# Differential scores and maxima map by map, layer 0's tiles in turn, the first tile of layer 1 projected in plain fp32

## The reference, cut to what matters

```python
branch = concat([mix, mem_o]) * silu(gate)          # block 1, layers A and B
x = x + branch @ w_out[i]
# block 2, layers 0 and 1
h  = rms(x, g_pre) * (1 + scale) + shift            # hc likewise, from the context
s1 = einsum('bqhd,bkhd->bhqk', q1, k1) * 48 ** -0.5 # 4 heads, 48 columns a map
s2 = einsum('bqhd,bkhd->bhqk', q2, k2) * 48 ** -0.5 # keys: 512 latent + 256 context
w  = softmax(s1) - lam * softmax(s2)
o  = einsum('bhqk,bkhe->bqhe', w, v)                # 96 columns a head
b_out = rms(o, subln_g) * (1 - lam_init)
y = concat([a_out * silu(na_g), b_out * silu(df_g), c_out * silu(cv_g)]) @ w_out
x = x + gate * rms(y, g_post)                       # context likewise in layer 0
```

## Time and profile before

| what | value |
|---|---|
| median of 3 runs | 1652.66 us (1650.25 to 1654.98) |
| profiled execution | 1653.44 us, of which the span is 1651.6 us |
| DMA | 161.36 MB, mean 98 GB/s |
| instructions | 22948 |
| largest groups of PE | L2596 575.2 us (x1696), 359.1 us (x1360), 224.5 us (x720) |
| projection in plain fp32, L3139 | 58.4 us (x128), mean 602 ns |

### The profile page before, as it was taken

One profiled execution on the slowest core, in us unless ns is written; L12 is line 12 of the kernel. 1 busy time (PEld: TensorE's weight loads), 2 busy tenths in 40 slices (PEclk: granted clock), 3 DMA queues, 4 the chain that ended last, 5 costly groups with the idle time before them and its releaser, 6 DMA issues.

```text
span 1651.6 us, 22948 instructions
## 1 busy us (share of the span) xinstructions
PE 1597.0 (97%) x8870; PEld 1277.7 (77%) x8870; DVE 979.8 (59%) x1803; ACT 667.6 (40%) x1323; POOL 140.7 (9%) x192
## 2 busy tenths in 40 slices
PE   7999999899999999999999999989999999999898
PEld 6977877687878878878888888865656887788676
DVE  1356454456556655665447787565665467876674
ACT  3365443424323323263313435244554325433653
POOL 4132100000000000002000110000112001000001
PEclk9999999899999999999999999999999999999899
DMA  8221244334654764462223111221003134213100
GB/s 289 81 77 50 103 153 117 80 82 121 190 158 120 155 185 139 148 151 68 92 96 109 56 54 40 92 93 58 1 26 96 48 107 140 58 39 128 52 14 39
DMA packets 171252, 161.36 MB, mean 98 GB/s; under 512 B 40374, under 2 KB 154280, under 8 KB 171112
## 3 DMA queue, kind: packets, MB, share of 16 engines
q1 hardware_dynamic: 151944, 126.97, 26.1%
q10 hardware_dynamic: 16928, 25.27, 4.7%
q0 software_dynamic: 2272, 7.64, 1.4%
HBM read 149.80 MB, written 11.18 MB: 97 GB/s over the span
## 4 chain that ended last, share of the span: by engine, by line
PE 83%; DVE 10%; ACT 4%; issue 2%; DMA 0%; POOL 0%; ACTq 0%; SPq 0%; POOLq 0%; DVEq 0%
PE psum L2596 46%; PE psum L2567 10%; PE psum L2630 7%; PE psum L3139 5%; PE psum L2621 4%; PE psum L3137 2%; PE psum L2775 2%; PE psum L2687 2%; PE psum L2730 2%; DVE arena L1999 1%; PE psum L2669 1%; PE psum L3010 1%; DVE arena L1969 1%; DVE wring_r L2076 1%; DVE arena L2133 1%
## 5 line engine op out<-in xcount | busy, mean ns | idle before, releaser
L2596 PE MATMUL psum<-hT_r,wring_r 128*128 128x512 f32 x1696 | 575.2, 393 | 3.6 <-ACT branch L1745 1.1
L2596 PEld LDWEIGHTS psum<-hT_r,wring_r 128*128 128x128 f32 x1696 | 319.3, 188 | 79.0 <-issue 10.0
L2596 PE MATMUL psum<-arena_r,wring_r 128*128 128x256 f32 (+1 forms) x1360 | 359.1, 333 | 0.7 <-ACT branch L1564 0.5
L1564 ACT ACTIVATE arena<-psum 128x512 f32<-128x512 f32 (+6 forms) x256 | 149.8, 611 | 416.0 <-PE psum L2596 244.2
L2596 PEld LDWEIGHTS psum<-arena_r,wring_r 128*128 128x128 f32 x1360 | 218.3, 190 | 26.2 <-issue 1.8
L2567 PE MATMUL psum<-arena 128*128 128x96 f32 (+9 forms) x1460 | 220.8, 365 | 16.9 <-ACT branch L1745 7.1
L2596 PE MATMUL psum<-arena_r 128*128 128x512 f32 (+1 forms) x720 | 224.5, 350 | 0.0
L2567 PEld LDWEIGHTS psum<-arena 128*128 128x128 f32 (+5 forms) x1460 | 160.8, 189 | 64.7 <-issue 31.9
L2596 PE MATMUL psum<-hT_r,arena_r 128*128 128x512 f32 x448 | 177.8, 397 | 1.8 <-DVE wring_r L2076 1.0
L2630 PE MATMUL psum<-ident,arena 128*128 128x128 f32 (+3 forms) x1104 | 145.9, 277 | 17.4 <-DMA arena<-in_c_ctx 7.4
L2630 PEld LDWEIGHTS psum<-ident,arena 128*128 128x128 f32 (+3 forms) x1104 | 125.2, 142 | 39.6 <-issue 14.6
(11 more groups left out here) (237 smaller groups left out, 1967.8 us busy)
## 6 DMA issues: line engine op xcount, KB each, us to landing
wring<-in_w_in_b SPq DMA_DIRECT2D x54, 512.0 KB, 5.9
arena<-in_w_mod ACTq DMA_DIRECT2D x16, 1536.0 KB, 8.3
wring<-in_w_in SPq DMA_DIRECT2D x16, 1536.0 KB, 6.9
wring<-in_w_out SPq DMA_DIRECT2D x8, 2048.0 KB, 8.4
wring<-in_w_in_a SPq DMA_DIRECT2D x5, 1536.0 KB, 6.6
arena<-x_dram SPq DMA_DIRECT2D x3, 2048.0 KB, 14.6
wring<-in_w_in SPq DMA_DIRECT2D x6, 1024.0 KB, 5.7
arena<-ebias_dram SPq DMA_DIRECT2D x144, 32.0 KB, 1.8
```

The lines of the kernel that those rows point to most:

```text
L1564: return nc.scalar.activation(out, in_, ACT.Copy, scale=scale)
L2596: ins_ = nc.tensor.matmul(b[0:hi.shape[2], 0:width], w[:, k], v[:, k], start=k + p == 0, stop=(k, p) == (KT - 1, 2))
```

## The change

The scores and the maxima of the differential stage are made map by map: PE claims the banks of a map and issues both parts of it, then the other map; DVE takes the maximum of the first map, combines the item before, and takes the maximum of the second map. Layer 0's tiles come in the order latent 0, context 0, latent 1, context 1, latent 2, latent 3. `oN` moves right behind what stands beside `dS`. `hcT 1` moves from behind `doT` of the last tile to behind `dT` of its last item. Layer 1's first tile is projected in plain fp32, so that its branch and its use of the split weights fall away; the splits of the output weights move from items 4 to 8 to items 8 to 11, two an item, and DVE's part of each waits until PE has read the plain weights for tile 0. `gate B 4` stands ahead of `qm B`, and `gate B 0` may start on the high parts. `nk` and `nkc` issue high by high and low by high before they wait for the state's low part. `final_rows(TT - 2)` gets a step of its own, `xr`, ahead of `hcT 0`. In layer 1 `nv` stands ahead of `nq`. The rooms of the first items' probabilities, the throwaway outputs of squares, the numbers of the norms and the allowed banks follow from the new order.

```diff
-YO_SPLITS = {4: ((0, 0), (0, 1)), 5: ((0, 3),), 6: ((0, 2), (1, 0)), 7: ((1, 1), (1, 3)), 8: ((1, 2),)}
+YO_SPLITS = {8: ((0, 0), (0, 1)), 9: ((0, 3), (0, 2)), 10: ((1, 0), (1, 1)), 11: ((1, 3), (1, 2))}
...
-    for i in range(4):
+    for i in range(5):
         add("a", "gate", "B", i)
     add("av", "qm", "B")
-    add("a", "gate", "B", 4)
     add("a" * 8, "mS", "B")
...
+    add("", "xr")
     add("vvvv", "hcT", 0)
     add("", "xf")
...
-        add(lat_ctx * 3, "nq", l)
+        if l == 0:
+            add(lat_ctx * 3, "nq", l)
         add("aaaavv", "nv", l)
+        if l:
+            add(lat_ctx * 3, "nq", l)
...
 def diff_tiles(l):
-    return ([TT + t for t in range(CT)] if l == 0 else []) + list(range(TT))
+    return [0, TT, 1, TT + 1, 2, 3] if l == 0 else list(range(TT))
+def turn_order(l):
+    return [("k", t) for t in (0, 1, TT, 2, 3, TT + 1)] + [("q", t) for t in diff_tiles(l)]
...
             add("a", "dT", l, t, h)
+            if n > len(items) and l == 0:
+                add("vvvv", "hcT", 1)
...
-            rows = [(tiles[i - 1], 1)] if h == 1 and i else [(t, 0)] if n == 5 or (h == DH - 1 and i) else []
+            rows = [(tiles[i - 1], 1)] if h == 1 and i else [(t, 0)] if h == DH - 1 and i else []
+            rows = [row for row in rows if row[0] != tiles[0]]
...
         beside(n)
+        if n >= 2 and h == 0 and i:
+            add("", "oN", l, tiles[i - 1])
...
         if n >= 2:
-            if h == 0 and i:
-                add("", "oN", l, tiles[i - 1])
...
-                if l:
+                if l and i > 1:
                     add("", "yb", tiles[i - 1], 1)
...
     add("v", "doT", l, last)
-    if l == 0:
-        add("vvvv", "hcT", 1)
-    else:
+    if l:
         add("", "yx", l, before)
...
                 elif kind == "yv":
                     dve.wait_ge(yo_w_hi, yo_ws.index((half, q)) + 1)
+                    read_by_pe(dve, ("yo", 1, 0, half, 1))
...
                 elif kind == "dS":                      # DVE
-                    if (t, h) != diff_items(l)[0]:
-                        diff_combine(n - 1)
                     for i in range(2):
                         full(dve, key, i)
                         chained(nc.vector.reduce_max(d_max[:, p, i:i + 1], halves(t, i), AX_XY if t < TT else AX_X))
                         scaled(d_neg[:, p, i:i + 1], d_max[:, p, i:i + 1], -diff_scale).then_inc(diff_negmax, 1)
+                        if i == 0 and (t, h) != diff_items(l)[0]:
+                            diff_combine(n - 1)
...
-                    for p, (w, v) in enumerate(((hi, x_hi), (hi, x_lo), (lo, x_hi))):
+                    if turned:
+                        pe.wait_ge(hi_ready, hi_at(turned, last_k))
+                        passes = ((hi, x_hi), (lo, x_hi), (hi, x_lo))
+                    for p, (w, v) in enumerate(passes):
+                        if turned and p == 2:
+                            evacuated(pe, turned, b_)
...
                     for k in range(KT):                  # nk
+                        pe.wait_ge(hi_ready, hi_at(("hT", f"C{l}"), k))
+                        for g, (hi, lo) in enumerate(parts):
+                            nc.tensor.matmul(banks[g], hi[:, k], hT_hi[:, k], start=k == 0, stop=False)
+                        for g, (hi, lo) in enumerate(parts):
+                            nc.tensor.matmul(banks[g], lo[:, k], hT_hi[:, k], start=False, stop=False)
                         evacuated(pe, ("hT", f"C{l}"), k)
                         for g, (hi, lo) in enumerate(parts):
+                            ins_ = nc.tensor.matmul(banks[g], hi[:, k], hT_lo2[:, k], start=False, stop=k == KT - 1)
...
-                    for half in range(2):                # dS, PE
-                        claim(pe, key, half)
...
-                        for part in range(2):
-                            cut = slice(part * KEYS // 2, (part + 1) * KEYS // 2)
-                            for half in range(2):
+                        for half in range(2):
+                            claim(pe, key, half)
+                            for part in range(2):
+                                cut = slice(part * KEYS // 2, (part + 1) * KEYS // 2)
                                 ins_ = product(psum[:, 2 * half + part, 0:KEYS // 2], [(q[half], dkT[rows[half], h, cut])])
-                                if part:
-                                    done(ins_)
+                            done(ins_)
...
-                    for k in yo_rows(t, piece) if l and not turned_last else ():
+                    for k in yo_rows(t, piece) if l and t and not turned_last else ():
...
-                    for k in yo_rows(t, piece) if l == 0 else ():
+                    for k in yo_rows(t, piece) if l == 0 or t == 0 else ():
                         ins_ = nc.tensor.matmul(b, src[:, k, tt * P:(tt + 1) * P], w[:, k], start=k == 0, stop=k == 5)
```

More of the change, by code:

```diff
@@ L277, in schedule @@
                     add("a", "cT", l, h)
-        turns = [("k", t) for t in (0, 1, TT, 2, 3, TT + 1)] + [("q", t) for t in diff_tiles(l)]
+        turns = turn_order(l)
         def turn(slot):
@@ L459, in turn_banks @@
         return range(BANKS - 1)
-    if key[2] == "k" or key[3] >= TT:
-        return range(BANKS - 1)
-    slot = (6 + key[3] + CT * (key[1] == 0)) // 2 + (key[0] == "dX")
+    slot = turn_order(key[1]).index(key[2:]) // 2 + (key[0] == "dX")
     return (range(BANKS - 1), (4, 5, 6), (4, 6))[max(slot, 4) - 4]
 def diff_tiles(l):
-    return ([TT + t for t in range(CT)] if l == 0 else []) + list(range(TT))
+    return [0, TT, 1, TT + 1, 2, 3] if l == 0 else list(range(TT))
+def turn_order(l):
+    return [("k", t) for t in (0, 1, TT, 2, 3, TT + 1)] + [("q", t) for t in diff_tiles(l)]
 def diff_items(l):
@@ L932, in hybrid_stack_kernel @@
         before_mem = split_at[("Bproj", 1, 0), 0]
-        split_starts = [("wout", "A"), ("wout", "B"), ("hcT", 1)]
+        split_starts = [("wout", "A"), ("wout", "B"), ("doT", 0, TT - 1)]
         split_bounds = [sum(split_jobs(key) for key, _ in steps[:order_of[start]]) for start in split_starts]
@@ L1120, in hybrid_stack_kernel @@
         for ph in norms:
[L1121 to L1125, removed]
+            if ph not in ("C0", "C1"):
+                tiles = {"F": FINAL_NORMS, "c1": NEXT_NORMS}.get(ph, [(ph, t) for t in range(norms[ph][2])])
+                for name, i in tiles:
+                    n_tiles += 1
+                    norm_no[name, i] = n_tiles
         norm_pe, n_tiles = {}, 0
@@ L1162, in yo_at @@
         def yo_at(l, t):
-            return t - TT if t >= TT else CT + t if l == 0 else TT + CT + t
+            return l * (TT + CT) + diff_tiles(l).index(t)
         def yo_rows(t, piece):
@@ L1567, in square @@
                 src, dst, _, ss, _ = norms[ph]
-                if ph == "c1":
-                    dst = cxn1
-                nc.scalar.activation(dst[:, t], src[:, t], ACT.Square, accum_out=ss[:, t:t + 1]).then_inc(sq_done, 1)
+                junk = cxn1[:, TT - 1] if ph == "c1" else dst[:, t]
+                nc.scalar.activation(junk, src[:, t], ACT.Square, accum_out=ss[:, t:t + 1]).then_inc(sq_done, 1)
             def final_squares(key, turns):
@@ L1936, in _ @@
                     b = full(act, key, 0)
-                    junk = cxn1[:, t % TT if l == 0 else 0]
+                    junk = cxn1[:, min(t, TT - 1) if l == 0 else 0]
                     nc.scalar.activation(junk[:, half * BANK:(half + 1) * BANK], b, ACT.Square,
@@ L2590, in split_features @@
                 for k in blocks:
+                    passes = ((hi, x_hi), (hi, x_lo), (lo, x_hi))
                     if key[0] == "nkc" and i == 0 and k % 2 == 0:
-                        evacuated(pe, ("hcT", key[1]), k // 2)
-                    if new and i == 0:
-                        evacuated(pe, new, k)
-                    for p, (w, v) in enumerate(((hi, x_hi), (hi, x_lo), (lo, x_hi))):
+                        turned, last_k, b_ = ("hcT", key[1]), k + 1, k // 2
+                    else:
+                        turned, last_k, b_ = new if i == 0 else None, k, k
+                    if turned:
[4 more added lines that the diff above has]
+                            evacuated(pe, turned, b_)
                         ins_ = nc.tensor.matmul(b[0:hi.shape[2], 0:width], w[:, k], v[:, k], start=k + p == 0, stop=(k, p) == (KT - 1, 2))
@@ L3121, in _ @@
                         pe.wait_ge(last_hi, 1)
-                    elif l:
+                    elif l and t:
                         pe.wait_ge(yo_x_lo, yo_xs.index((t, piece)) + 1)
```

13 lines of the change are left out of this document (7 added, 6 removed).

## The result

The changed kernel takes 1664.05 us (median of 9 runs, 1658.97 to 1669.25) against 1653.73 us before (9 runs); the ratio is 1.006, 95% interval 1.0047 to 1.0073. The forecast was 1650, its range ended at 1661: outside the range, and on the other side. The profiled execution has a span of 1662.9 us, 11.3 more than before.

A forecast was written before the change was run, and what follows sets the result against it. PE, busy 97% of the span, was taken to bound the kernel. The terms -10.4 - 0.3 - 1.8 + 1.1 + 3.0 + 1.7 - 0.7 + 5.2 gave -2.2 us; forecast 1650 us, eight-in-ten range 1638 to 1661.

The forecast's parts named there:

- Parts 1 and 2: `gate B 4` ahead of `qm B`: -10.4 us; `nk` starting on the high parts with `xr` first, layer 0: -1.8 us.
- R4: Rival at `mS B`: the gate's eviction still meets the split in ACT's queue, `mS` waits as before; 1661 us, chance 0.04.
- Part 3: Scores and maxima map by map in the differential stages: no gain in PE's work, `oN` 1.46 us later.
- R3: Rival in the differential stages: PE runs the maps one after the other; +35 us, 1685 us, chance 0.03.
- part 4: Layer 0's differential stage with its tiles in turn, a latent tile first: +1.1 us, bounds -4 to +5.
- part 7: Layer 1's differential stage, four pieces summed: +5.2 us, bounds -3 to +9.
- (c): Layer 1's stage: DVE's weight splits, two an item in items 8 to 11, make PE wait through item 12: +4.5 us.
- Part 5: `hcT 1` in layer 0's last item delays the eviction before `yo 3`: +3.0 us and +1.7 of clock.
- Part 6: Layer 1 before the stage: `nv` ahead of `nq` gives DVE time for the splits: -0.7 us, bounds 0 to -1.5.
- (b): Layer 1's first tile in plain fp32: 0.69 us more a piece, +2.1 us beyond the piece counted in the first items.
- (a): Layer 1's first items without the splits: -4.4 us, less 1.5 for the combination before the fourth item's dT.
- R2: Rival in both stages' first items: DVE's order decides and its waits bring the clock down; about +6, 1659 us, chance 0.21.

## Why the prediction was wrong

By stretches of the profiled executions, in us against the kernel before:

| stretch | forecast | changed kernel | with DVE's old order |
|---|---|---|---|
| up to the first scores | -12.5 | -11.3 | -12.4 |
| layer 0's stage | +1.1 | +5.2 | -1.6 |
| to layer 1's first scores | +4.0 | +5.2 | +3.1 |
| layer 1's stage | +5.2 | +10.7 | -2.3 |
| the end | 0 | +1.5 | +0.1 |
| sum | -2.2 | +11.3 | -13.0 |

Each column is one execution. In the eight kernels that have the changed kernel's steps up to there the first scores of layer 0 start between 1064.63 and 1068.07 us, so 2 or 3 us in the first row say nothing.

**Parts 1 and 2 were right.** `nk 0` is 12.0 us earlier; 12.5 were forecast. R4 is out.

**Part 3 is the step that failed: it put the late combination at nothing where no projection fills PE.** Half of the mechanism stood in the text: DVE's combination now stands between the maxima, `oN` comes 1.46 us later, PE waits for it at a boundary of layer 1. The wait is 1.1 to 1.4 us. PE's side stood too: eight score records take 1.57 us map by map where they took 1.56 in turn, so the row groups overlap and R3 is out. What failed is the step "Where nothing fills PE (the first items) the loop takes 4.8 to 4.9 us by this working as before", and the sum that followed. The starts of the scores are 4.97 us apart in the changed kernel, as written. But map by map the start says only that the first map's banks are free. The second map starts 1.28 us later, and PE goes on when that is done. From the start of one item's scores to the end of the next one's it is 6.52 us before, 6.43 with the claims map by map and DVE as before, and 7.81 in the changed kernel (the rows of layer 0's stage above, at the higher level). With the claims together the starts show it as well: 6.34 instead of 4.96. Either way the order takes 1.3 to 1.4 us an item there, one wait of 1.10 us for the combination ahead of `dT` and one for the second map's exponential.

The forecast counted 1.5 us for the whole of layer 1's first items; they cost 8.9 (the first seven items take 57.99 us against 49.14 with the old order), of which the clock is 6.8: 13.7 us at the lower level against none. In layer 0 I wrote "1.0 at the boundaries" where a tile costs 1.48, because I followed `oN` and not `yx` and what waits behind it. The terms that name this order are 3.0 us in part 4 and 1.5 and 1.5 in part 7, in all 6.0; the 4.5 of part 7 (c) are for the splits with this order behind them. It measured 23.5.

**Part 4** was counted with the order in it. Without it layer 0's stage gains 1.6 us, in a profile without the 6.8 us at the lower level of the kernel before, which are worth 3.4.

**Part 5 was right**: 3.3 us of wait were forecast, 3.47 came. `nk 1` was to come 4.7 us later, the clock included; it does with DVE's old order (52.78 us from the last scores, 48.04 before), and 6.8 in the changed kernel. That the sum fits to 0.1 is luck: in that profile the lower level stretched the eight records behind the wait from 3.60 to 6.38 us, 2.8 where 1.7 were forecast, so 2 are left of the 3.0. Against `hcT 1` behind `doT` it cost 5.4.

**Part 6** is open: 0.7 forecast, 1.6 measured between `nk 1` and the scores (229.41 us against 230.97). But of the ten other kernels with `nv` ahead of `nq` four took 229.3 to 229.4 us there and six 230.9 to 231.2, so one execution doesn't show what this edit is worth.

**Part 7**: (b) is 0.69 us for each plain piece, as worked out (the pitch is 7.09 and not 6.40). Items 7 to 15 lose 7.7 us, where the three pieces of (b) that are left, (c) and (d) had 2.1 + 4.5 + 1.5 = 8.1; what was missed is the same 1.5 us once more behind the last tile. With DVE's old order they lose only 3.6, so more than half of the 7.7 is the order again. (a) is what failed: the first items were to gain 2.9 us and lost 3.0. With DVE's old order they gain 5.9, of which 5.1 is clock.

R2 named the mechanism (DVE's order decides, and its waits bring the clock down) at 1659, with a chance of 0.21. It was short as well: it priced the clock and not the waits, and in layer 0's stage the clock stayed up. Still it was nearer. The sum priced a late combination only where a tile ends, though the profile before had 12 us of PE's waits and 8.5 of lost clock in the two stages, most of them in the first items, where PE stands behind DVE and ACT.

## What to carry to other kernels

- When a reduction and the finishing pass of the item before share an engine, the finishing pass goes first: its user is the next thing that the busiest engine asks for, and it can run while the new scores are being made. Put between the two maxima, in 40 items, it cost 23.5 us here; put behind both, 5 more.
- Price a changed order of one engine against every instruction behind it in its queue, in each regime of the loop (filled, unfilled, boundary), and each half of a double edit alone. Take the pitch of a loop from where its last part ends: where a step may start on half of its banks, the distance of the starts looks like "no change".
- Try parts apart: the edits at the front gave 15.5 us, and two lines of DVE's order took more than that back.

## What was not expected of the hardware

- The clock doesn't follow a moved wait in a fixed way. In layer 1's stage DVE's order took the time at the lower level from 0 to 13.7 us in the changed kernel, and from 10.2 to 13.7 in the kernel before. The changed kernel fell at 1530.8 after waits of 0.52, 0.45 and 1.10 us, and the kernel with DVE's old order stayed at the higher level in this stage with waits of 0.52, 0.17, 0.24, 0.99 and 0.73 us. These are single executions: over the nine of the changed kernel the mean granted clock lies between 0.989 and 0.997 and the time between 1658.97 and 1669.25 us. What decides it is left open.
- `oN` (0.56 us) stands in DVE's queue behind two maxima and a combination and started at 1593.28, though PE's last product ahead of it had ended at 1587.33. The Trainium skill ("Perfetto Trace Analysis", Tensor Engine Instruction (MATMUL, LD_WEIGHTS)) calls ACT and DVE strict FIFO; the trace agrees.
- Scores of the two row groups overlap whichever way they are issued: the records of a pair start 6 or 7 ns apart in turn and 13 or 14 ns apart map by map. They overlap only if both maps may start: where the second map starts 0.9 or 1.3 us later, eight records take 2.46 or 2.83 us at the higher level.
